# Finishing a tile in later turns of the scores stage: index sums, normalisation and pair transposes of a product-key retrieval

## What is computed

```python
q = (xb @ w_pq).reshape(128, 8, 256)
s1 = einsum('thd,kd->thk', q[..., :128], sub_keys1)
s2 = einsum('thd,kd->thk', q[..., 128:], sub_keys2)
v1, i1 = top_k(s1, 16)
v2, i2 = top_k(s2, 16)
cand = (v1[..., :, None] + v2[..., None, :]).reshape(128, 8, 256)
cidx = (i1[..., :, None] * 128 + i2[..., None, :]).reshape(128, 8, 256)
top_s, sel = top_k(cand, 16)
eidx = take_along_axis(cidx, sel, axis=-1)
g = softmax(top_s)
```

## Time and profile before

| | us |
|---|---|
| median of 3 runs (lowest, highest) | 4264.05 (4262.37, 4265.49) |
| the profiled execution | 4265.55 |
| its span in the trace | 4263.8 |
| busy: TensorE, VectorE, ScalarE, GpSimd | 3824.2, 3000.0, 1239.7, 1742.4 |

### The profile page before, as it was taken

One profiled execution on the slowest core, in us unless ns is written; L12 is line 12 of the kernel. 1 busy time (PEld: TensorE's weight loads), 2 busy tenths in 40 slices (PEclk: granted clock), 3 DMA queues, 4 the chain that ended last, 5 costly groups with the idle time before them and its releaser, 6 DMA issues.

```text
span 4263.8 us, 58819 instructions
## 1 busy us (share of the span) xinstructions
PE 3824.2 (90%) x19146; PEld 3098.8 (73%) x19146; DVE 3000.0 (70%) x6037; ACT 1239.7 (29%) x1869; POOL 1742.4 (41%) x1065
## 2 busy tenths in 40 slices
PE   8899776999569888466999999999989999999998
PEld 1799743666555344245999999998979999999997
DVE  0322244333443888887999999998888888888888
ACT  0410132222221222055333333333323223333222
POOL 0222000000320222201555555555557777777775
PEclk9799886999679899755999999999999999999999
DMA  7389600666332000036999999999999999999997
GB/s 244 119 271 289 226 0 20 185 205 201 114 116 83 30 31 32 6 133 247 318 330 340 330 330 341 323 337 339 346 331 340 339 338 345 331 346 342 335 344 273
DMA packets 302316, 1017.99 MB, mean 239 GB/s; under 512 B 30394, under 2 KB 61916, under 8 KB 294932
## 3 DMA queue, kind: packets, MB, share of 16 engines
q1 hardware_dynamic: 155348, 489.04, 34.2%
q0 software_dynamic: 127584, 481.35, 31.1%
q10 hardware_dynamic: 19296, 46.67, 2.8%
HBM read 875.22 MB, written 141.72 MB: 239 GB/s over the span
## 4 chain that ended last, share of the span: by engine, by line
PE 51%; DVE 1%; DMA 1%; issue 0%; POOL 0%; ACT 0%; ACTq 0%; POOLq 0%; DVEq 0%
PE p_y L2121 24%; PE p_a L2102 8%; PE p_a L2101 8%; PE p_a L2105 8%; PE next_pw L1729 2%; DMA rows<-u_rows,pairsT 0%; DMA h_lo<-h_spill 0%; DVE rows L2043 0%; DMA rows<-in_v,pairsT 0%; DVE p_y L2087 0%; DVE h_lo L2073 0%; POOL rows L1990 0%; DVE h_rows L2079 0%; DVE h_hi L2071 0%; DVE x1g L2090 0%
## 5 line engine op out<-in xcount | busy, mean ns | idle before, releaser
L1990 POOL DMA_INDIRECT rows<-in_v,pairsT x384 | 756.9, 1971 | 283.7 <-DVE h_rows L2056 194.4
L1990 POOL DMA_INDIRECT rows<-u_rows,pairsT x384 | 632.1, 1646 | 481.8 <-DVE pairsT L2043 409.3
L2101 PE MATMUL p_a<-h_hi,u_hi 128*128 128x384 f32 x2048 | 689.5, 337 | 40.8 <-DVE h_lo L2073 39.4
L2102 PE MATMUL p_a<-h_lo,u_hi 128*128 128x384 f32 x2048 | 692.9, 338 | 0.0
L2121 PE MATMUL p_y<-v_hi,g_hi 128*128 128x512 f32 x1536 | 487.3, 398 | 0.0
L1958 ACT ACTIVATE v_hi<-v_raw 128x1024 fp32r<-128x1024 f32 x256 | 272.0, 1063 | 729.8 <-PE p_y L2121 721.9
L2121 PE MATMUL p_y<-v_lo,g_hi 128*128 128x512 f32 x1536 | 475.9, 391 | 0.0
L2056 DVE SCALAR_TENSOR_TENSOR h_rows<-rows,pairsT,h_rows 128x1024 f32<-128x1024 f32 x381 | 466.8, 1279 | 4.8 <-DMA rows<-in_v,pairsT 3.5
L2043 DVE CUSTOM_DVE_ANT_0 rows<-rows,h_rows 128x1024 f32<-128x1024 f32 x384 | 450.5, 1220 | 24.4 <-DMA rows<-u_rows,pairsT 24.3
L2101 PEld LDWEIGHTS p_a<-h_hi,u_hi 128*128 128x128 f32 x2048 | 386.7, 189 | 51.9 <-DVE h_lo L2073 40.1
L2105 PE MATMUL p_a<-h_hi,u_lo 128*128 128x384 f32 x2048 | 398.1, 335 | 2.0 <-DVE u_lo L2018 2.0
(11 more groups left out here) (302 smaller groups left out, 5849.1 us busy)
## 6 DMA issues: line engine op xcount, KB each, us to landing
u_raw<-in_uT SPq DMA_DIRECT2D x256, 512.0 KB
v_raw<-in_v SPq DMA_DIRECT2D x256, 512.0 KB
w_ring<-weights_spill POOLq DMA_DIRECT2D x32, 1536.0 KB
u_rows<-pairsT ACTq DMA_DIRECT2D x64, 512.0 KB
key_cols<-in_uT SPq DMA_DIRECT2D x64, 512.0 KB, 4.1
u_rows<-key_rows SPq DMA_DIRECT2D x64, 512.0 KB
wada<-in_w_ada SPq DMA_DIRECT2D x12, 2048.0 KB, 7.9
weights_spill<-first_wt SPq DMA_DIRECT2D x24, 1024.0 KB
```

The lines of the kernel that those rows point to most:

```text
L1990: pool.indirect_dma_start(rows[s][n % SLOTS][:], None, (keep.u_rows, v_rows)[g], at).then_inc(rows_in[s][n % SLOTS], 16)
L2101: nc.tensor.matmul(p_a[:, 0:GT], u_hi[s][:, k, :], h_hi[:, k, :], start=k == 0, stop=False)
L2102: nc.tensor.matmul(p_a[:, 0:GT], u_hi[s][:, k, :], h_lo[:, k, :], start=False, stop=False)
```

## The change

The two waits, the sums and the normalisation move out of `weights` into a new function `finish`, which `sort(t)` calls for tile t - 1 after `first_sort(t)`. The three transposes of `pairs` of tile t - 3 stand in turn t, between `project` and `scores`. The copy into `keep.pairsT` goes from VectorE to ScalarE (`keep_pairs`), `exps` is for tile t - 2 and stands ahead of `norm`, and `mix_columns` stands behind `norm`. `transpose_mix` stands between the second and the third bank of the scores. The one-hot tables lie in the first two rows of `keep.mix`, whose contents have been copied by then. Two more turns are written out ahead of the loop.

```diff
-    hot = tuple(sc2[:].rearrange("p g k -> p (g k)").bitcast(BF16)[:, n * 2 * D:(n + 1) * 2 * D].rearrange(
-        "p (h k c) -> p h k c", h=PEER_HEADS, k=TOPK) for n in range(2))
+    hot = tuple(keep.mix[:, n, :].bitcast(BF16).rearrange("p (h k c) -> p h k c", h=PEER_HEADS, k=TOPK) for n in range(2))
+    READ = 3
...
-            with eng.Fori(1, TILES - 2) as t:
+            for t in range(1, READ):
+                turn(t)
+            with eng.Fori(READ, TILES - 2) as t:
                 turn(t)
...
 # TensorE, transpose_mix
-                else:
-                    wait_count(pe, hs_full, t - 1)
+                elif not (isinstance(t, int) and t == 0):
+                    pe.wait_ge(hs_full, t - 1)
+                    pe.wait_ge(pairs_read, t - 1)
...
             def pairs_to_columns(t):
                 pe.wait_ge(pairs_full, t + 1)
-
-                pe.wait_ge(mT_full, min(t + 4, TILES) if isinstance(t, int) else t + 4)
-                pe.wait_ge(pairs_read, t + 1)
+                pe.wait_ge(hs_full, min(t + READ + 1, TILES) if isinstance(t, int) else t + (READ + 1))
+                pe.wait_ge(pairs_read, t + READ)
...
                 if projects:
                     project(t + 1)
+                if not isinstance(t, int) or t >= READ:
+                    pairs_to_columns(t - READ)
+                pe.wait_ge(hs_full, t + 1)
+                wait_count(pe, sc_full, t)
+                scores(t, (0, 1))
                 if transposes:
                     transpose_mix(t + 2)
-
-            in_turns(pe, columns, scores, before, pairs_to_columns)
+                scores(t, (2, 3)).then_inc(psc_full, 1)
+
+            in_turns(pe, columns, lambda t: None, before, lambda t: None)
+            for t in range(TILES - READ, TILES):
+                pairs_to_columns(t)
...
 # ScalarE
             def exps(t):
                 act.wait_ge(e_in, t + 2)
+                act.wait_ge(pt_full, t + 1)
                 nc.scalar.activation(pairs[:, 2], best[:], ACT.Exp).then_inc(e_out, 1)
+
+            def keep_pairs(t):
+                act.wait_ge(pt_full, t + 2)
+                nc.scalar.activation(keep.pairsT[:, :, bass.ds(t * P, P)], pT[:, 0:3, :], ACT.Copy).then_inc(pairs_read, 1)
...
                 modulated(t)
+                if not isinstance(t, int) or t >= READ:
+                    keep_pairs(t - READ)
+                if not isinstance(t, int) or t >= 2:
+                    exps(t - 2)
+                if projects:
+                    norm(t + 1)
                 if transposes:
                     mix_columns(t + 2)
-                if projects:
-                    norm(t + 1)
...
 # VectorE
+            def finish(t):
+                dve.wait_ge(pt_full, t + 1)
                 for s in range(2):
                     dve.wait_ge(picked, t * 2 + s + 3)
                     last = nc.vector.reduce_sum(pairs[:, s], hot[s], AX.X)
...
                 nc.vector.tensor_tensor(pairs[:, 2], pairs[:, 2], sums[:, 1, :].unsqueeze(2).to_broadcast([P, PEER_HEADS, TOPK]), ALU.mult).then_inc(pairs_full, 1)
-                dve.wait_ge(pt_full, t + 2)
-                nc.vector.tensor_copy(keep.pairsT[:, :, bass.ds(t * P, P)], pT[:, 0:3, :]).then_inc(pairs_read, 1)
...
                 first_sort(t)
+                if not first:
+                    finish(t - 1)
                 if projects:
                     gated_rows(t + 2)
```

More of the change, by code:

```diff
@@ L1351, in stage_scores @@
     waited = sem("sort_waited")
-    LINKS = 17
+    LINKS, LATE = 17, 3
     xv = a["x"].rearrange("(t p) d -> t p d", p=P)
@@ L1470, in transpose_h, with scores @@
                 last.then_inc(ht_full, 1)
[L1472 to L1475, removed]
+            def scores(t, banks):
+                for b in banks:
                     for k in range(KD):
                         last = nc.tensor.matmul(psc[:, 4 * b:4 * b + 4, :], hs[:, k, :], wc[:, k, 4 * b:4 * b + 4, :], start=k == 0, stop=k == KD - 1)
-                last.then_inc(psc_full, 1)
+                return last
             def pairs_to_columns(t):
                 pe.wait_ge(pairs_full, t + 1)
-                pe.wait_ge(mT_full, min(t + 4, TILES) if isinstance(t, int) else t + 4)
-                pe.wait_ge(pairs_read, t + 1)
+                pe.wait_ge(hs_full, min(t + READ + 1, TILES) if isinstance(t, int) else t + (READ + 1))
+                pe.wait_ge(pairs_read, t + READ)
                 for n in range(3):
@@ L1562, in columns @@
                 modulated(t)
+                if not isinstance(t, int) or t >= READ:
[4 more added lines that the diff above has]
+                    norm(t + 1)
                 if transposes:
                     mix_columns(t + 2)
-                if projects:
-                    norm(t + 1)
[L1568 to L1573, removed]
+            act.sem_inc(pairs_read, READ)
+            in_turns(act, columns, keep_scores, before, lambda t: None)
+            keep_pairs(TILES - 3)
+            exps(TILES - 2)
+            keep_pairs(TILES - 2)
             exps(TILES - 1)
+            keep_pairs(TILES - 1)
         @block.vector
@@ L1578, in _ @@
             link = Links(dve, dve_t)
-            dve.sem_inc(pairs_read, 1)
             def gated_rows(t):
@@ L1612, in weights @@
             def weights(t):
-                dve.wait_ge(pt_full, t + 1)
                 link(nc.vector.tensor_copy(sums[:, 0, :], best[:, :, 0]))
@@ L1658, in sort @@
             def sort(t, projects=True):
-                link.at(t * LINKS)
+                first = isinstance(t, int) and t == 0
+                link.at(0 if first else t * LINKS - LATE)
                 first_sort(t)
+                if not first:
+                    finish(t - 1)
                 if projects:
@@ L1666, in sort @@
                 weights(t)
-                assert link.n == LINKS, link.n
+                assert link.n == LINKS - (LATE if first else 0), link.n
             gated_rows(0)
@@ L1675, in _ @@
             reciprocal_norm(1)
-            with dve.Fori(0, TILES - 2) as t:
+            dve.wait_ge(mx_full, 2)
+            sort(0)
+            with dve.Fori(1, TILES - 2) as t:
                 sort(t)
@@ L1679, in _ @@
             sort(TILES - 1, False)
+            link.at(TILES * LINKS - LATE)
+            finish(TILES - 1)
 class WeightSteps:
```

## The result

| | before | after |
|---|---|---|
| median of 4 runs each (lowest, highest), us | 4263.21 (4259.55, 4265.49) | 4199.25 (4197.49, 4201.58) |
| span of the profiled execution, us | 4263.8 | 4195.7 |

The ratio is 0.9851, 95% interval 0.9834 to 0.9868: 64 us faster, where 56 were forecast (4263.21 - 4207).

A forecast was written before the change was run, and what follows sets the result against it. In the scores stage a closed loop of VectorE's sort with four pauses set the 53.00 us turn. Eight steps saving 12.93 and paying 5.30, less 0.2 and 2.8, gave 58.0 us: 4207 us, range 4200 to 4224.

The forecast's parts named there:

- VectorE's turn of 45.4: Scores stage loop: a turn falls from 53.00 us by 7.63 net (12.93 removed, 5.30 back in `finish`).
- Sort 1 late by 2.8: Start of the scores stage: sort 1 waits for tile 1's scores and begins 2.8 us late.
- Cover of 11.7 us: GpSimd's multiplications end 8 us into the next sort, needed only at its cast, 19.7 us in; uncovered price 5.7 us a turn.
- Nothing for GpSimd beside MAX8 and FIND_INDEX8: `first_sort`: 8 us of GpSimd multiplications beside these VectorE instructions cost nothing; far end 8 us x 8.
- The rival of a held first sort: GpSimd holds VectorE in `first_sort`, 8 us in each of eight sorts: 4271 us, no change; chance 0.04, partial hold 0.02.
- TensorE has 2.1 us of pause: Scores stage loop: TensorE's full-clock turn takes 43.3 us, so it idles 2.1 us in a turn of 45.4.
- The rival in which TensorE or ScalarE takes the lead: Scores stage: thin slacks of 3.6 and 1.8 us are eaten; 4212 us at 46.3 us a turn, 4225 at 48; chance 0.14.
- That the low clock doesn't return: Scores stage: TensorE's clock at or near 1.0; rival of staying at 1.2 GHz, near 4500 us, chance 0.01.
- the number: Whole kernel: 4265.55 - 58.0 = 4207.5, or 4206.0 from the median of 4264.05; 4207 us taken.
- doesn't see the change: Experts stage, 2265 us: unaffected, since it starts after a barrier and reads the same data.
- theory A: From the experiments: stretches ahead of and behind the scores stage scatter from execution to execution, whatever the kernel.
- B: From the experiments: the change itself shortens the stretches ahead of and behind the scores stage; 63 to 65 us apart in total.

The follow-up runs named there:

- the held one: Changed kernel with 25 idle VectorE reductions behind the last one of the scores stage, so that later stages start at about their old time: 4257.75 us.

## Why the prediction was wrong

The direction and the mechanism were right, and the stage came out at 57.7 us for a sum of 58.0. Point by point:

- *VectorE's turn of 45.4*: 45.43 in every profile of the change. *Sort 1 late by 2.8*: 2.92. *The last tile's waits stay open*: they are the only 5.7 us for GpSimd that the waits show, of 51.1; 8.2 us more work came back as 8.2 us.
- *Cover of 11.7 us*: shown by the two runs with added multiplications, one on each side of it.
- *Nothing for GpSimd beside MAX8 and FIND_INDEX8*: shown by their durations beside up to 20 us of multiplications. The rival of a held first sort falls. The trace agrees for MAX8 and FIND_INDEX8 with the rule that the prediction takes from the Trainium skill ("SBUF — State Buffer", Who interferes with whom). One thing in the first sort can be held, its cast (1.09 us for 0.29 beside GpSimd's copy, with one input), but only with four multiplications added; so the prediction's reason, one input, is not the whole of it.
- *TensorE has 2.1 us of pause*: 1.94; 1.7 us of added work closed it at no cost to the turn, and 6.9 us made TensorE lead at 50.15 for a forecast of 50.2. The rival in which TensorE or ScalarE takes the lead falls for this kernel. Its working has a small slip: 39.5 + 1.15 + 1.02 + 43.3 + 1.88 is 86.9 and not 87.2, which changes nothing. That the low clock doesn't return was right in most turns; where it did, its 1.7 us were taken out of the next pause.

**The step that failed is "the number"**, and with it the low end of the range. It has two terms that were wrong.

First, the time from which 58.0 was taken. With 4207 the prediction started from 4265 (4207 + 58), between one execution of 4265.55 us and what a median of three gave. The six medians of the kernel before, of 4 to 21 runs each, are 4260.0 to 4263.2, mean 4261.1. This is 3.9 us of the miss. Single executions of that kernel reached from 4256.65 to 4265.33 us in 21 runs, and the one that was profiled lies above all of these.

Second, that the experts stage "doesn't see the change": every stage but one was put at nothing. (The 2265 us given for that stage are a window that begins 14 us into it; it takes 2279.4.) By the prediction's own sign, a change of that stage by more than a few us, this was wrong in the first pair of profiles: 2279.4 and 2273.2. The kernel before alone moved to 2276.3 in its second profile, so one pair can't settle it, but the runs together can. I take each run's median less its own stage, which is what all else takes; the stage repeats to 0.05 us. For the kernel before this gives 3790.0 to 3793.2 us in six medians. Twelve runs have the two written-out turns and no work added on TensorE (for the held one its 56.7 us are taken off too): they give 3786.5 to 3790.4. Each of the twelve lies below the kernel before that was measured beside it, by 0.1 to 6.3 us, 2.9 on average. So theory A is right about the scatter, and B about some 3 us that belong to the change and lie outside its stage. The two runs that have the written-out turns and nothing else lie 2.8 and 3.6 us below, so this part of the change may be enough for it. The profiles point to the experts stage without settling it: 2275.5 to 2279.4 us in the four of the old order (2275.5 in both with written-out turns), 2272.9 to 2274.8 in nine of the twelve of the new order and 2275.6 to 2279.4 in the other three. By what mechanism written-out turns of one stage would shorten a later one stays open.

With both, 4261.1 - 57.7 - 3 = 4200.4; the three medians of the changed kernel are 4199.25, 4202.88 and 4198.91. The remaining microsecond is scatter, and so is on which side of 4200 the measured median fell: the second one lies inside the range. The low end of 4200 left 7 us below the number, just what the base and the other stages took. That an earlier start speeds up the later stages was tested and isn't so.

## What to carry to other kernels

Where several engines meet at one point of a loop, write the loop as a few inequalities between their clocks, each with its slack; here that gave the turn to 0.1 us, and said beforehand that three turns of delay suffice and two don't. A wait moved behind other work is free exactly as long as the cover lasts, so compute the cover and not only the wait. And take a saving off a median of many runs, with some microseconds in the range for the stages that it isn't meant to touch: a sum good to 0.3 us in its own stage was worth only some 7 us in the whole. When a few microseconds are in question, subtract from each run the stage whose length repeats, and compare the rest over all runs.

## What the runs showed of the hardware

- In the run with four more multiplications a cast of VectorE from uint32 to bf16 of 256 elements took 1.09 us in the five turns in which a 1.04 us copy by GpSimd lay beside it, and 0.29 us in the four in which none did, though it has one input. The instructions of the first sort were not held there: beside GpSimd's multiplications and without them the median is 275 and 275 ns for MAX8 and 285 and 284 ns for FIND_INDEX8. Nor were the reductions.
- Two f32 additions of VectorE with two inputs took 3.30 us beside GpSimd's residual and 1.15 us without it.
- In one of two like turns a pause of TensorE of 1.93 us was followed by a stretch at 1.2 GHz, and in the other, of 1.94 us, not. With the pause split in 0.98 and 0.78 us the granted clock was 1.00 in the whole loop. With 12.74 us in one piece it fell to 1.2 GHz in every turn.
